# First normalisation of a diffusion block with channels on the partitions instead of tokens

## What is computed

```python
def _rms_norm(x, gain):
    xf = x.astype(jnp.float32)
    y = xf * lax.rsqrt(jnp.mean(xf * xf, axis=-1, keepdims=True) + EPS)
    return (y * gain.astype(jnp.float32)).astype(x.dtype)

def _modulate(h, shift, scale):
    return h * (1.0 + scale) + shift
...
        mod_x = jax.nn.silu(c) @ w_ada[l] + b_ada[l]
        mod_c = jax.nn.silu(c_ctx) @ w_ada[l] + b_ada[l]
...
        h_x = _modulate(_rms_norm(x, norm1_gain[l]), sh1, sc1)
        h_c = _modulate(_rms_norm(ctx, norm1_gain[l]), csh1, csc1)
```

## Time and profile before

| | us |
|---|---|
| median of 3 runs | 1274.28 |
| lowest and highest | 1273.71, 1274.79 |
| span of the profiled execution | 1273.3 |
| TensorE busy (matmul) | 1247.7 |
| VectorE busy | 884.7 |
| ScalarE busy | 610.2 |
| GpSimd busy | 163.1 |

### The profile page before, as it was taken

The page is one execution under the profiler, slowest core; times in us unless marked ns, Lnnn a source line. Parts: engine busy times, 40 slices in busy tenths (PEclk is TensorE's granted clock), DMA queues, the critical chain, the costliest instruction groups (busy, mean ns, idle before and its releaser), DMA issues.

```text
span 1273.3 us, 16935 instructions
## 1 busy us (share of the span) xinstructions
PE 1247.7 (98%) x6216; PEld 1030.8 (81%) x6216; DVE 884.7 (69%) x1392; ACT 610.2 (48%) x1039; POOL 163.1 (13%) x112
## 2 busy tenths in 40 slices
PE   5999999999999999999999999999999999999997
PEld 3788788888988878888888888888888888888886
DVE  5572577758659987877688665565555669768866
ACT  7761211235436433443677555555545433654444
POOL 0125330142260000025510000000000000000000
PEclk9999999999999999999999999999999999999999
DMA  9414220103276456496732644444448985477534
GB/s 368 181 33 154 78 100 2 34 20 100 69 274 230 141 202 211 161 365 234 265 133 88 200 166 143 149 164 142 140 156 281 320 292 183 159 236 256 193 105 160
DMA packets 95226, 219.18 MB, mean 172 GB/s; under 512 B 11532, under 2 KB 11932, under 8 KB 95144
## 3 DMA queue, kind: packets, MB, share of 16 engines
q1 hardware_dynamic: 82752, 182.70, 42.2%
q10 hardware_dynamic: 8728, 22.29, 4.7%
q0 software_dynamic: 3664, 13.11, 3.2%
HBM read 166.66 MB, written 51.39 MB: 171 GB/s over the span
## 4 chain that ended last, share of the span: by engine, by line
PE 81%; DVE 7%; DMA 6%; issue 2%; ACT 2%; POOL 1%; SPq 1%; ACTq 0%; DVEq 0%
PE ps L2988 13%; PE ps L2990 13%; PE ps L2989 13%; PE ps L3607 8%; PE ps L3599 8%; PE ps L3602 8%; DMA raw<-in_w_stream 3%; PE ps L3625 3%; PE ps L3437 3%; PE ps L3442 3%; PE ps L3439 3%; PE ps L3029 2%; PE ps L3071 1%; POOL ring_lo L1051 1%; PE ps L3224 1%
## 5 line engine op out<-in xcount | busy, mean ns | idle before, releaser
L2988 PE MATMUL ps<-t_hi,s_hi 128*128 128x512 f32 x392 | 153.4, 391 | 0.1
L2989 PE MATMUL ps<-t_lo,s_hi 128*128 128x512 f32 x392 | 153.1, 391 | 0.0
L2990 PE MATMUL ps<-t_hi,s_lo 128*128 128x512 f32 x392 | 153.1, 391 | 0.0
L1792 ACT ACTIVATE s_hi<-s_raw 128x512 fp32r<-128x512 f32 x112 | 70.5, 630 | 114.0 <-DMA b<-in_w_stream 58.4
L1051 POOL TENSOR_TENSOR ring_lo<-raw,ring_hi 128x1024 fp32r<-128x1024 f32 (+2 forms) x37 | 86.2, 2342 | 207.1 <-ACT ring_hi L1177 203.4
L2867 DVE TENSOR_TENSOR s_lo<-s_raw,s_hi 128x512 fp32r<-128x512 f32 x112 | 77.3, 690 | 42.3 <-ACT s_hi L1792 41.8
L2988 PE MATMUL ps<-ring_hi,hT_hi 128*128 128x512 f32 x224 | 91.4, 408 | 0.0
L2990 PE MATMUL ps<-ring_hi,hT_lo 128*128 128x512 f32 x224 | 87.7, 391 | 0.0
L2989 PE MATMUL ps<-ring_lo,hT_hi 128*128 128x512 f32 x224 | 87.5, 391 | 0.0
L2988 PEld LDWEIGHTS ps<-t_hi,s_hi 128*128 128x128 f32 x392 | 73.6, 188 | 16.2 <-DVE t_lo L2871 0.5
L2990 PEld LDWEIGHTS ps<-t_hi,s_lo 128*128 128x128 f32 x392 | 73.7, 188 | 15.9
(11 more groups left out here) (509 smaller groups left out, 3201.7 us busy)
## 6 DMA issues: line engine op xcount, KB each, us to landing
s_raw<-ff_scr SPq DMA_DIRECT2D x112, 256.0 KB, 2.8
raw<-in_w_stream SPq DMA_DIRECT2D x34, 512.0 KB, 3.9
ff_scr<-ffs SPq DMA_DIRECT2D x16, 1024.0 KB, 4.8
t_raw<-in_w_stream SPq DMA_DIRECT2D x64, 256.0 KB, 3.4
w_B_raw<-in_w_stream SPq DMA_DIRECT2D x48, 256.0 KB, 2.8
ff_scr<-ffa SPq DMA_DIRECT2D x16, 768.0 KB, 4.5
b<-in_w_stream SPq DMA_DIRECT2D x48, 256.0 KB, 4.5
ada_next<-in_ada_columns POOLq DMA_DIRECT2D x13, 512.0 KB, 3.8
```

What stands on the lines that cost most here:

```text
L1792: A(s_slot[n][0][:], s_slot[n][2][:], ACT.Copy).then_inc(down_hi, 1)
L2988: M(dst, lhsT=l_hi, rhs=r_hi, start=first, stop=False, skip_group_check=goes_on)
L2989: M(dst, lhsT=l_hi, rhs=r_lo, start=False, stop=False, skip_group_check=goes_on)
L2990: return M(dst, lhsT=l_lo, rhs=r_hi, start=False, stop=last, skip_group_check=goes_on)
```

## The change

The host now lays out all ten tiles with channels on the partitions (`x_columns`: partition = channel within a block, free dimension = block, then token), so no tile is transposed on the core. The sum of squares over channels is made in two steps: ScalarE squares the tile without its accumulator, VectorE adds the eight blocks (`tokens_squares`, a reduction with a stride of 128 elements, result 128 by 128), and TensorE multiplies this with a 128x128 matrix of ones (`square_total`), which leaves every token's sum on all partitions. Mean, root and reciprocal are therefore 128 columns wide (`ms_w`, `rt_w`, `rstd_w`, two buffers each). The scaling by the reciprocal moves from ScalarE to GpSimd (`scale`), as a multiplication of the tile with `rstd_w` spread over the eight blocks. The modulations of VectorE and ScalarE read the tile in SBUF instead of PSUM. The x tiles that the last residual needs come from `x` as before. Some semaphores are shared with later users, whose counts get an offset (`N_TILES`, `N_FIRST`, `N_SECOND`).

```diff
+        def squares(s):
+            return by_channel(junk[:]) if s < EARLY else h_raw[:, :, SEQ - P:SEQ]
+
+        def sums_bank(s):
+            return 2 + s % 2
...
         def load_x(eng, s):
-            src = ins["ctx"][s * P:(s + 1) * P, :] if s < 2 else ins["x"][(s - 2) * P:(s - 1) * P, :]
-            eng.dma_start(x_tile(s), src).then_inc(x_landed[s], 16)
+            eng.dma_start(x_tile(s), ins["x_columns"][s]).then_inc(x_landed[s], 16)
...
+            def scale(s):
+                pool.wait_ge(rstd_ready, s + 1)
+                x = by_channel(x_tile(s))
+                nc.gpsimd.tensor_tensor(x, x, rstd_w[:, s % 2, None, :].to_broadcast([P, KT, P]), ALU.mult
+                                        ).then_inc(xhat, 1)
+
+            scale(0)
+            scale(1)
             lo(INDEX[("k", 0)])
+            for s in range(2, EARLY):
+                scale(s)
             pool.wait_ge(split, INDEX[("k", 2)])
-            for i in range(INDEX[("k", 2)], INDEX[("q", 2)]):
+            for i in range(INDEX[("k", 2)], INDEX[("v", 0)]):
+                lo(i)
+            for s in range(EARLY, 9):
+                scale(s)
+            for i in range(INDEX[("v", 0)], INDEX[("v", 2)]):
+                lo(i)
+            scale(9)
+            for i in range(INDEX[("v", 2)], INDEX[("q", 2)]):
                 lo(i)
...
                 if s:
-                    act.wait_ge(sumsq, s)
-                if s < EARLY:
-                    dst, src = junk[:], x_tile(s)
-                else:
-                    dst = h_raw[:, :, SEQ - P:SEQ]
-                    src = x_tile(s).rearrange("p (c t) -> p c t", c=KT)
-                A(dst, src, ACT.Square, accum_out=ss[:, s:s + 1]).then_inc(sumsq, 1)
+                    act.wait_ge(sq_summed, s)
+                A(squares(s), by_channel(x_tile(s)), ACT.Square).then_inc(sumsq, 1)
 
             def root_of(s):
                 act.wait_ge(meansq, s + 1)
-                A(rt[:, s:s + 1], ms[:, s:s + 1], ACT.Sqrt).then_inc(root, 1)
-
-            def norm(s):
-                act.wait_ge(rstd_ready, s + 1)
-                A(x_tile(s), x_tile(s), ACT.Identity, scale=rstd[:, s:s + 1]).then_inc(xhat, 1)
+                A(rt_w[:, s % 2, :], ms_w[:, s % 2, :], ACT.Sqrt).then_inc(root, 1)
...
             def tokens_mean(s):
 
+                dve.wait_ge(sq_total, s + 1)
+                V.tensor_scalar(ms_w[:, s % 2, :], ps[:, sums_bank(s), 0:P], 1.0 / D, EPS, ALU.mult, ALU.add
+                                ).then_inc(meansq, 1)
+
+            def tokens_rstd(s):
+
+                dve.wait_ge(root, s + 1)
+                if s >= 2:
+                    dve.wait_ge(xhat, s - 1)
+                V.reciprocal(rstd_w[:, s % 2, :], rt_w[:, s % 2, :]).then_inc(rstd_ready, 1)
+
+            def tokens_squares(s):
+
                 dve.wait_ge(sumsq, s + 1)
-                V.tensor_scalar(ms[:, s:s + 1], ss[:, s:s + 1], 1.0 / D, EPS, ALU.mult, ALU.add).then_inc(meansq, 1)
...
+                if s >= 2:
+                    dve.wait_ge(sq_total, s - 1)
+                V.tensor_reduce(sq_sum[:, s % 2, :], squares(s).rearrange("p c t -> p t c"), AX.X, ALU.add
+                                ).then_inc(sq_summed, 1)
...
-                    ins_ = V.tensor_scalar(dst[:, q, :], ps[:, side_bank(key), q * P:(q + 1) * P], a1[:, c, r:r + 1],
+                    ins_ = V.tensor_scalar(dst[:, q, :], x_tile(n)[:, c * P:(c + 1) * P], a1[:, c, r:r + 1],
                                            mod[:, c, r:r + 1], ALU.mult, ALU.add)
...
+            def square_total(s):
+
+                pe.wait_ge(sq_summed, s + 1)
+                if s >= 2:
+                    pe.wait_ge(meansq, s - 1)
+                M(ps[:, sums_bank(s), 0:P], lhsT=ones[:], rhs=sq_sum[:, s % 2, :], start=True, stop=True
+                  ).then_inc(sq_total, 1)
...
             for kt in range(KT):
                 ada_part(0, kt)
+                if kt == 4:
+                    square_total(0)
+                if kt == 6:
+                    square_total(1)
...
             for n in range(EARLY):
-                k_part(n, 1, ("hh", "lh", "hl"), lambda: x_transposes(n + 3, (1,) if n < 2 else (0, 1)) if n < 3 else None)
-            x_transposes(6)
+                k_part(n, 1, ("hh", "lh", "hl"), lambda: square_total(5 + n // 2) if n % 2 == 0 else None)
             for s in range(EARLY, 10):
                 main(("k", TILES[s]), lambda: k_transposes(s - 5))
-                if s + 2 < 10:
-                    x_transposes(s + 2)
+                if s + 3 < 10:
+                    square_total(s + 3)
```

102 lines of the change are left out of this document (49 added, 53 removed).

## The result

The changed kernel takes 1308.01 us (median of 4 runs, 1307.72 to 1309.34) against 1274.1 for the kernel before in the same comparison: ratio 1.0261, 95% interval 1.0249 to 1.0273, so 33.9 us slower. The forecast was 1292 with a range of 1280 to 1301. The direction was right, the size about half of what came, and the time lies outside the range.

The account below looks back on a forecast made before the run. TensorE, busy 1247.7 of 1273.3 us, was taken as the bound. Delays of 13.5 us up to the second row transposes and 3.9 from there to v made +17.4 on 1274.3: 1291.7, say 1292, range 1280 to 1301.

Parts of the forecast that it names:

- D: From second row transposes to first product on v: -6.2 transposes saved, +1.0 products with ones, +9.1 stops, sum +3.9 us.
- the walk: Each queue's new order set against estimated durations, 0.06 us per handover; over the old order it gave 95.1 against 95.06.
- the port wait: VectorE instructions reading SBUF wait until GpSimd's running instruction is over; rival without this wait: 1284 us, 20%.
- the stops at the five products with ones: Second half, tiles 5 to 9: TensorE loses 2.6, 2.8, 0.9, 0.7 and 2.1 us, 9.1 in sum.
- A: Up to the first product on k: 23.87 becomes 26.5, +2.6 us.
- give the port up after each, +2.0: Four modulations each giving the port up to GpSimd: +2.0 us, 1294, counted inside the forecast.
- B: Up to the first product on tile 2: 31.67 becomes 37.7, +6.0 us in all.
- C: Up to the second row transposes: 40.12 becomes 53.6, +13.5 us in all, TensorE waiting since 46.0.
- The ring: Before the second row transposes, per tile: modulation, rounding, root, reciprocal, scaling in sequence, 5.4 us with handovers.
- The clock: TensorE's lower clock after the stop before the second row transposes: 1.65 us, mostly swallowed by the next stop; 1 at most.
- The saving: Twenty groups of transposes off TensorE, 8.8 us; rival with every stop covered: -7.2, 1267 us, 4%.
- the dear sum: Rival: VectorE's strided sum takes 2.3 us instead of 1.23; first product on v 7.3 later, 1299 us, 12%.

Follow-up runs that it names:

- e9: The kernel before without its groups of x transposes, modulations reading two fixed PSUM banks written once by eight transposes: 1273.36 us, ratio 0.9986.
- e4: The kernel after, with matmuls that nobody reads (fillers) put into TensorE's stops in both halves: 1302.25 us, ratio 1.0215.

## Why the prediction was wrong in size

The step that failed is the pricing of four terms, each too low: the modulations beside GpSimd (0.8 us, up to 5.2 measured, 4.1 us at D), the strided sum (1.23, 1.9 measured, 4.4 us at D), TensorE's clock behind its stops ("by 1 at most", 5.8 us at D) and, with it, the wait of the other engines for TensorE's products with ones, which the walk put at nothing.

What held: TensorE waits for others early, and the change pays nothing there. The reciprocal (0.95), the mean (0.29 against 0.26), the root (0.31 against 0.27), the port wait as a kind, the places of the long stops, and even the stops at the five products with ones: 9.1 us forecast, 10.6 measured (2.63 and 2.70 for tiles 5 and 6, forecast 2.6 and 2.8).

**A, +2.6 forecast, +5.3 measured.** The step that failed is "gets the port at 25.0, ends at 25.8". The copy of the rows (to 21.94, forecast 22.1) and the scalings (to 25.57, forecast 25.0) were right. But the four modulations did not pass together: the first ended with the second scaling, the second with the remainder of weights, and only then the other two passed, so that the first rounding began at 28.50. With the modulations in PSUM A is 25.73. I had the alternative in the text, that the four "give the port up after each, +2.0", and left it inside the forecast as a fringe. Where nothing holds them, four take 1.11 us and not 0.8, and a scaling takes 2.34 and not 2.1.

**B, +6.0 forecast, +9.0 measured.** 2.7 of this are those of A, little is its own. The reduction took 1.96 instead of 1.23, but the mean behind it had to wait 1.34 us more for TensorE, whose product with ones (33.59) stood behind twelve products on tiles 0 and 1 that took 4.4 us. With the contiguous sum this wait was 3.21 and B no earlier; with fillers B came 1.5 us earlier. The missing link is TensorE here already.

**C, +13.5 forecast, +19.3 measured.** The ring of 5.4 us per tile was measured at 5.5 for tile 3 (scalings at 36.37 and 41.89), and 7.9 for tile 4 (49.76). The missing link is again TensorE: its product with ones of tile 4 stands behind twelve products on tile 2, which ran at 1.2 GHz. The fillers show it, 3.2 us at C. To this comes tile 4's modulation, 5.16 us.

**D, +3.9 forecast, +13.3 measured.** The stops were right in size, the other terms not. TensorE's busy time was to fall by 5.2 and rose by 2.6, 7.8 us of slow products behind the stops. But the clock is not the whole price of it: fillers there gave back 1.9, since a tile lasts 8 to 10 us on VectorE and not 6.6. Of that the stride is 0.7, and the contiguous sum gave 4.4; the rest is two ropes between two reductions and, at tile 9, ScalarE's square. The forecast's sum also has a slip of its own: 17.4 us put D at 112.5, the walk (105.0 + 8.1) at 113.1.

**The clock.** "It moves the forecast by 1 at most" was wrong by a factor of six. I had argued that the next stop would swallow the slow products. It does so only where nothing that ends the next stop depends on them, and here a sum of squares stood behind them in the queue.

**The saving.** "From 23.87 on it never stops, so whatever shifts the last landmark shifts the end" is true of delays, and I used it for savings as well. e9 shows how close behind TensorE the others were, in the old arrangement: of 6.2 us of transposes taken out behind C, stops gave back 3.1. The busy shares (VectorE 34.09, ScalarE 40.01 of 54.94 us) had looked like room. I had checked my walk against the old order, but never walked the old order without its transposes.

**The range.** The two cheapest-to-name errors, the dear sum (12%, 1299) and the clock, were held apart as rivals of which one comes true. They added up: stride and clock give 9.2 us together at D, and the port another 4.1 in a run of its own. These are 13.3 of the 14.6 us that D was beyond my 113, if the port's share adds as the other two did; that combination with the original order was not run. With the prices that my text had for them (7.3 for the sum, 2.0 for the modulations, 1.6 for the scaling, 1 for the clock), all at once, the range would have reached 1304; what is then missing, 4.4 us, is about what the clock took beyond my 1.

What stays open: whether the port's share adds to the other two, and what freeing ScalarE of the scalings is worth by itself.

## What to carry to other kernels

An engine at 100% in the profile says what a delay there costs, not what taking work from it gives; time a variant without the work before building its replacement. When unknown prices all push in one direction, put them all at their dear end at once for the range. And a stop of TensorE can cost twice: once idle, once in the slow products behind it (in the kernel after behind those of 2.07 to 8.22 us, not behind that of 1.86), whose price must be followed through every wait that stands behind them in its queue.

## What was unexpected in the hardware

- A fp32 reduction over eight elements 128 apart took 1.925 us for 1024 elements a partition, over eight neighbours 1.205.
- Four VectorE instructions of 0.28 us each that read SBUF took 5.16 us beside two GpSimd instructions (4.63 in all), and 3.1 beside one. One of them passed when a GpSimd instruction was over, and the next waited for the next one (2.35, 2.37, 0.33 and 0.33 us). A scaling on GpSimd that began beside VectorE's remainder took 3.40 instead of 2.34 and ended 2.25 us behind it.
- Eight fp32r products of 128 columns took 0.84 us from start to start, 0.11 each, no less than transposes of that size (0.11).
- The granted clock read 0.50 behind stops of 6.6 and 8.2 us, 0.50 also behind one of 2.07 (43 to 46 us) and 0.57 behind one of 2.6 (69.8 to 73.8 us), but 1.00 behind one of 1.86 (98.4 to 101.0 us). With idle matmuls in the stops it read 1.00 behind them (e4, 29 to 31 us and all of C to D). Whether the transposes did a part of this service in the kernel before is not shown: e9, with 0.50 from 24 to 28 us where the kernel before reads 1.00, has eight transposes at that place as well, and stopped 2.22 us instead of 1.34 ahead of it.
